# One tile of a 31-tap convolution given to GpSimd, the bias products put among the modulation sums, and another order in the router

## The reference

```python
mod = c_act @ w_ada[l] + b_ada[l]                    # six modulation vectors
u = modulate(rmsnorm(h, g_norm1[l]), sh1, sc1)
y = hybrid_mixer(u, w_in[l], ...)                    # the first mixer
h = h + ga1[:, None, :] * y
u2 = modulate(rmsnorm(h, g_norm2[l]), sh2, sc2)
y2 = hierarchical_moe(u2, ...)

# in hybrid_mixer: a depthwise convolution of 31 taps over 512 channels
a, gt = jnp.split(u, 2, axis=-1)
z = a * jax.nn.sigmoid(gt)
z = lax.conv_general_dilated(z, w_dw, window_strides=(1,), padding=[(CONV_WIDTH - 1, 0)], ...) + b_dw
z = jax.nn.silu(layernorm(z, ln_g, ln_b))

# in hierarchical_moe: 4 groups of 8 experts, the best group, then its best 2 experts
lg = t @ w_rg + b_rg
_, gsel = lax.top_k(lg, 1)
le_sel = jnp.take_along_axis(le, gsel[:, :, None], axis=1)[:, 0, :]
top_v, top_i = lax.top_k(le_sel, TOP_K)
for e in range(N_EXPERTS):
    hid = jax.nn.silu(t @ w1[e]) * (t @ w3[e])
    y = y + comb[:, e:e + 1] * (hid @ w2[e])
```

## Time and profile before

| | before |
|---|---|
| runs | 1441.7 us (1437.92 to 1446.5, three runs) |
| the profiled execution's own time | 1443.55 us |
| its span | 1441.7 us |
| mean granted TensorE clock | 0.92 |
| TensorE, VectorE, ScalarE, GpSimd busy | 1199.7, 675.6, 449.9, 2.2 us |
| read from device memory | 372.03 MB |

### The profile page before, as it was taken

One profiled execution on the slowest core, in us unless ns is written; L12 is line 12 of the kernel. 1 busy time (PEld: TensorE's weight loads), 2 busy tenths in 40 slices (PEclk: granted clock), 3 DMA queues, 4 the chain that ended last, 5 costly groups with the idle time before them and its releaser, 6 DMA issues.

```text
span 1441.7 us, 20119 instructions
## 1 busy us (share of the span) xinstructions
PE 1199.7 (83%) x8634; PEld 947.6 (66%) x8634; DVE 675.6 (47%) x1146; ACT 449.9 (31%) x643; POOL 2.2 (0%) x16
## 2 busy tenths in 40 slices
PE   5999998897865657555675599999998889899998
PEld 2789896686322223222231399899998889899986
DVE  2547987453200101101010464455657786678974
ACT  2543343442000000000000353343545454545453
POOL 0000000000000000000000000000000000000000
PEclk7799999999989879888788999899999999999999
DMA  9797862977999999999999565343443425345552
GB/s 355 253 317 241 278 165 89 360 253 304 420 420 420 420 420 418 420 421 420 420 420 415 201 213 183 108 133 118 148 161 116 142 93 193 115 158 182 190 203 88
DMA packets 169655, 374.48 MB, mean 260 GB/s; under 512 B 8263, under 2 KB 121305, under 8 KB 145881
## 3 DMA queue, kind: packets, MB, share of 16 engines
q1 hardware_dynamic: 167040, 369.55, 69.5%
q0 software_dynamic: 144, 3.54, 0.8%
q10 hardware_dynamic: 2376, 0.04, 0.1%
HBM read 372.03 MB, written 4.62 MB: 261 GB/s over the span
## 4 chain that ended last, share of the span: by engine, by line
PE 58%; DMA 21%; DVE 11%; SPq 5%; ACT 3%; issue 3%; DVEq 0%; ACTq 0%
PE bank L603 31%; DMA arena<-in_w 15%; PE bank L1231 4%; DVE arena L1262 4%; DMA above<-in_w 4%; PE bank L907 4%; SPq L2599 4%; DVE fine L1254 2%; PE bank L947 2%; ACT fine L2059 2%; DVE arena L1254 2%; PE bank L563 2%; PE bank L600 2%; PE bank L634 1%; DVE arena L1259 1%
## 5 line engine op out<-in xcount | busy, mean ns | idle before, releaser
L603 PE MATMUL bank<-fine 128*128 128x256 f32 x4512 | 564.6, 287 | 17.8 <-DVE fine L1254 17.7
L603 PEld LDWEIGHTS bank<-fine 128*128 128x128 f32 x4512 | 554.3, 195 | 31.9 <-issue 27.8
L1254 DVE TENSOR_TENSOR fine<-arena,fine 128x1024 fp32r<-128x1024 f32 (+2 forms) x263 | 299.6, 1168 | 181.5 <-ACT fine L2059 172.1
L2059 ACT ACTIVATE fine<-arena 128x1024 fp32r<-128x1024 f32 (+2 forms) x279 | 266.3, 984 | 197.5 <-PE bank L603 82.4
L2059 ACT ACTIVATE arena<-bank 128x256 f32<-128x256 f32 (+2 forms) x153 | 68.2, 473 | 523.9 <-PE bank L919 191.7
L907 PE MATMUL bank<-arena 128*32 128x512 f32 x640 | 121.6, 790 | 62.8 <-DMA arena<-in_w 41.2
L1254 DVE TENSOR_TENSOR arena<-arena,bank 128x512 f32<-128x512 f32 x8 | 8.4, 1052 | 286.7 <-PE bank L907 286.7
L907 PE MATMUL bank<-above,arena 128*32 128x512 f32 x384 | 75.1, 724 | 51.6 <-issue 21.6
L2059 ACT ACTIVATE arena<-arena 128x512 f32<-128x512 f32 (+6 forms) x90 | 61.1, 708 | 152.1 <-DVE arena L1262 62.2
L907 PEld LDWEIGHTS bank<-arena 128*32 128x32 f32 x640 | 30.4, 140 | 118.9 <-issue 117.3
L1262 DVE SCALAR_TENSOR_TENSOR arena<-arena 128x256 f32<-128x256 f32 (+3 forms) x262 | 107.7, 484 | 1.1 <-ACT arena L2059 0.8
(11 more groups left out here) (177 smaller groups left out, 784.5 us busy)
## 6 DMA issues: line engine op xcount, KB each, us to landing
arena<-in_w SPq DMA_DIRECT2D x118, 1024.0 KB, 26.8
above<-in_w SPq DMA_DIRECT2D x66, 1024.0 KB, 26.5
arena<-in_w_in SPq DMA_DIRECT2D x62, 1024.0 KB, 5.5
arena<-in_w_ada SPq DMA_DIRECT2D x24, 1024.0 KB, 9.8
arena<-in_ffn_w_up SPq DMA_DIRECT2D x22, 1024.0 KB, 5.1
arena<-in_ffn_w_down SPq DMA_DIRECT2D x11, 1024.0 KB, 5.0
arena<-in_w_ada_f SPq DMA_DIRECT2D x8, 1024.0 KB, 10.6
above<-in_w SPq DMA_DIRECT2D x12, 512.0 KB, 18.5
```

Of the source, the lines that this page charges most:

```text
L603: ins = e.matmul(o, w[:, k, j * P:j * P + P], x[:, kt, :], start=start, stop=stop, skip_group_check=True)
L1254: return e.tensor_tensor(o, a, b, f)
L2059: return e.activation(o, i, f, bias=bias, scale=scale)
```

## The change

Three parts. First, `conv_taps` on VectorE has three tiles in place of four, and GpSimd makes the fourth with a product into `rstd` and an addition for each tap. Its DMA of the bias rows stands behind all of that, and TensorE waits for both engines ahead of the layer norm. Second, the router's products are put in another order, the count is made with two instructions ahead of the gather and two behind it, and the wait of L907 is for each quarter of `xg`. Third, the bias products move ahead of `ada_sums(3)`, with their copies and store on ScalarE, and `oh` is loaded with 33 partitions into the place of `u`, between the fourth and the fifth piece of the modulation weights.

```diff
-        oh = shaped(flat(v)[:, 0:1152], 3, 384)
+        oh = shaped(flat(u)[:, 0:1152], 3, 384)
...
             ada_sums(2)
-            ada_sums(3)
-            ada_to_mod(0)
-            advance("q", 2)
             e.wait_ge(*cols_in["first"])
             e.wait_ge(*oh_in[0])
...
                 e.matmul(bank[0:6, 0:384], rtab[0:33, 6 * g:6 * g + 6], oh[0:33, g, :], start=True,
                          stop=True).then_inc(*rep_made.up(g))
+            ada_sums(3)
+            ada_to_mod(0)
+            advance("q", 2)
...
             e.wait_ge(*conv["taps"])
+            e.wait_ge(*conv_g["taps"])
...
-            e.wait_ge(*squares["most"])
-            e.matmul(bank[:, 0:256], ones, sq[:, 0, :], start=True, stop=False)
             e.wait_ge(*route["wr"])
             raw_logits(0)
             raw_logits(1)
+            e.wait_ge(*squares["most"])
+            e.matmul(bank[:, 0:256], ones, sq[:, 0, :], start=True, stop=False)
...
             turn_h(0, 0)
+            turn_h(0, 1)
             bank = misc(route_a, "rstd")
...
-            turn_h(0, 1)
...
-            e.matmul(bank[:, 0:32], before, mask[:, 0, :], start=True, stop=True)
-            e.matmul(bank[:, 32:64], ones, mask[:, 0, :], start=True, stop=False)
-            e.matmul(bank[:, 32:64], before, mask[:, 1, :], start=False, stop=True)
-            e.matmul(bank[:, 64:96], ones, mask[:, 0, :], start=True, stop=False)
-            e.matmul(bank[:, 64:96], ones, mask[:, 1, :], start=False, stop=True).then_inc(*router.up("ranks"))
+            e.matmul(bank[:, 0:64], before, flat(mask), start=True, stop=False, skip_group_check=True)
+            e.matmul(bank[:, 32:64], ones, mask[:, 0, :], start=False, stop=True, skip_group_check=True).then_inc(*router.up("ranks"))
...
             gather_tokens(0, (0,))
+            e.matmul(bank[:, 64:96], ones, mask[:, 0, :], start=True, stop=False, skip_group_check=True)
+            e.matmul(bank[:, 64:96], ones, mask[:, 1, :], start=False, stop=True, skip_group_check=True).then_inc(*router.up("count"))
...
-                            e.wait_ge(*gathered[quad, th])
+                            e.wait_ge(*gathered[quad, th, 0])
                         for k in range(4):
+                            if wn == 0 and k:
+                                e.wait_ge(*gathered[(quad, th, k) if k < 3 else (quad, th)])
...
                 for j in range(1, 31):
-                    for m in range(4):
+                    for m in range(3):
...
+            e.wait_ge(*out_v["a", 1])
+            e.wait_ge(*fills["zp"])
+            e.tensor_scalar(cacc[:, 3, :], zp[:, 3, 0:256], col("w_dw", 3 * 31), col("b_dw", 3), ALU.mult, ALU.add).then_inc(
+                *conv_g.up(0))
+            for j in range(1, 31):
+                e.wait_ge(*conv_g[j - 1])
+                e.tensor_scalar(rstd, zp[:, 3, j:j + 256], col("w_dw", 3 * 31 + j), None, ALU.mult).then_inc(
+                    *conv_g.up(("product", j)))
+                e.wait_ge(*conv_g["product", j])
+                e.tensor_tensor(cacc[:, 3, :], cacc[:, 3, :], rstd, ALU.add).then_inc(
+                    *conv_g.up(j if j < 30 else "taps"))
             e.wait_ge(*row_out[0])
             e.wait_ge(*scores[2, 1])
...
             for j in range(4):
                 ada(j)
+                if j == 1:
+                    e.dma_start(flat(oh)[0:33, :], T["consts"][0:33, NCONST0 + NCONST1:NCONST]).then_inc(*oh_in.up(0, 16))
             load("q", 2)
-            e.wait_ge(*ada_sum[4])
-            e.dma_start(flat(v)[:, 0:1152], T["consts"][:, NCONST0 + NCONST1:NCONST]).then_inc(*oh_in.up(0, 16))
```

More of the change, by code:

```diff
@@ L477, in build @@
             "ffn_silu", "down_x_hi", "ends_by_scalar"))
-        fills = signal("fills")
+        fills, conv_g = signal("fills"), signal("conv_taps_by_gpsimd")
         x_turned, norm_sum, ada_sum, ada_mod, rep_made, products_of, small_made, scores, kd_turned, states, ln_sum, o_made, on_turned, conv_out = (
@@ L1505, in conv_taps @@
                 for j in range(1, 31):
-                    for m in range(4):
+                    for m in range(3):
                         e.wait_ge(*conv[m, j - 1])
                         stt(cacc[:, m, :], zp[:, m, j:j + 256], col("w_dw", m * 31 + j), cacc[:, m, :], ALU.mult, ALU.add).then_inc(
-                            *conv.up((m, j) if j < 30 or m < 3 else "taps"))
+                            *conv.up((m, j) if j < 30 or m < 2 else "taps"))
                     yield
@@ L1689, in gather_tokens @@
                         k = 4 * g + j
-                        ins = ts(xg[:, i, k, :], bank_of(gathered, (quad, g))[:, j * P:j * P + P], perm[:, 0, k:k + 1], ALU.mult,
-                                 perm[:, 1, k:k + 1], ALU.add)
-                    ins.then_inc(*gathered.up((quad, g)))
+                        ts(xg[:, i, k, :], bank_of(gathered, (quad, g))[:, j * P:j * P + P], perm[:, 0, k:k + 1], ALU.mult,
+                           perm[:, 1, k:k + 1], ALU.add).then_inc(*gathered.up((quad, g, j) if j < 3 else (quad, g)))
             e.wait_ge(*perm_in[0])
@@ L1710, in vector_program @@
             step(e.tensor_copy(rank, shaped(ranks[:, 0:64], 2, 32)))
+            e.wait_ge(*router["count"])
             step(e.reduce_max(cnt[:, 0:1], ranks[:, 64:96], AX), "count")
@@ L2177, in scalar_program @@
             norm_rows(0, lambda pair: h_in[1, pair // 2])
+            for g in range(3):
+                e.wait_ge(*rep_made[g])
+                act(rep[0:6, g, :], bank_of(rep_on, g)[0:6, 0:384], ACT.Copy).then_inc(*rep_on.up(g))
+            e.wait_ge(*rep_on[2])
+            e.dma_start(bass.AP(scratch.tensor, P * rows, [[384, 6], [6 * 384, 3], [1, 384]]), rep[0:6, :, :]).then_inc(
+                *row_out.up(0, 16))
             high_half()
@@ L2187, in scalar_program @@
             advance("q", 1)
-            for g in range(3):
-                e.wait_ge(*rep_made[g])
-                act(rep[0:6, g, :], bank_of(rep_on, g)[0:6, 0:384], ACT.Copy).then_inc(*rep_on.up(g))
-            e.wait_ge(*rep_on[2])
-            e.dma_start(bass.AP(scratch.tensor, P * rows, [[384, 6], [6 * 384, 3], [1, 384]]), rep[0:6, :, :]).then_inc(
-                *row_out.up(0, 16))
             e.wait_ge(*ada_sum[7])
```

## The result

The changed kernel takes 1456.72 us (median of 4 runs, 1453.22 to 1461.76), the kernel before 1440.16 (4 runs, 1437.92 to 1446.5). The ratio is 1.0095, 95% interval 1.0067 to 1.0122: **0.7 to 1.2% slower**. The forecast was 1433 us, with a range up to 1449. The profiled execution took 1456.19 us, its span 1454.4, against 1441.7: 12.7 us more.

A forecast was written before the change was run, and what follows sets the result against it. Expert weight loads set the time from 360 us, so earlier savings pass on one to one. Start -3.0, mixer -2.3 and router -3.6 sum to -8.9: 1434.65 us profiled, 1433 predicted as median, range 1426 to 1449.

The forecast's parts named there:

- To land by then it must be issued by 169.7: Mixer: bias-row copy behind GpSimd's chain costs nothing if issued by 169.7 us, before ScalarE's store at 183.97.
- the hold: Convolution: time by which GpSimd's instructions lengthen VectorE's, h us per product-and-addition pair; forecast near 0.41.
- the case with a chance of 0.10: Mixer rival: GpSimd too slow, its copy late; at 1.2 us per instruction store 17 late, +8, 1443 us; chance 0.10.
- the one with 0.27: Mixer rival: GpSimd holds VectorE up for its instructions' length; 1439 us at h 0.62, 1447 at 0.89; chance 0.27.
- The signs that the prediction named: Mixer: TensorE's waits above 15 us mean GpSimd holds VectorE; GpSimd's DMA behind 170 us means its copy is late.
- The mixer: Convolution: VectorE loses 31 instructions, gain 4.5 us if GpSimd hinders nobody; half taken, 2.3 us saved, range -4.5 to +12.
- The formula 30h - 14.7: Convolution: mixer's net change in us if each GpSimd pair holds VectorE up for h us; never below -4.5.
- the 7.5 us of free time: Convolution: VectorE's free time from 113.6 to 141.5 us, expected to absorb 7.5 us of GpSimd's hindrance.
- 9 us in hand: Mixer: TensorE, up to three halves of 3 us behind, absorbs 9 us of the late store, leaving +8.
- The start: Bias products moved earlier let L563 run unbroken, with an earlier clock rise: 3.0 us saved, bounds 0.7 to 5.4.
- the clock rises at 48.3: Start: before, TensorE's clock rose some 4.8 us after L563 ran unbroken from 43.48; now expected near 43.0.
- The router: Before the experts: squares 1.8, count 1.3, single scalings 0.6 us; 3.6 of 3.7 us saved, bounds 1.9 to 4.0.

The follow-up runs named there:

- run 10: Kernel before, all four tiles on VectorE, nothing computed by GpSimd; only its copy of the bias rows waits for level 3's last tap: 1456.51 us, ratio 1.0095.
- run 2: Changed kernel with GpSimd's copy of the bias rows issued ahead of its tap 14, not behind tap 30: 1439.2 us, ratio 0.9979.
- run 1: Changed kernel with all four convolution tiles back on VectorE, new start and router kept: 1435.49 us, ratio 0.9958.
- run 4: Kernel before with only the fourth tile moved to GpSimd and the copy issued ahead of the 14th pair: 1446.73 us, ratio 1.0034.
- run 6: Kernel before, all taps on VectorE; GpSimd also computes the fourth tile's 61 instructions into free tiles, copy after its 13th pair: 1460.96 us, ratio 1.0137.
- run 7: Kernel before, all taps on VectorE; GpSimd also runs 61 chained clearings of free tiles, which read nothing: 1443.2 us, ratio 1.0.
- run 8: Kernel before with only the start's part of the change: 1442.24 us, ratio 0.9996.
- run 3: Kernel before with only the fourth tile moved to GpSimd and the copy behind its 61 instructions: 1466.11 us, ratio 1.016.
- run 5: Changed kernel with ScalarE's store going to its own piece of scratch, so that it waits for no copy: 1457.22 us, ratio 1.0109.
- run 11: Kernel before, all taps on VectorE, GpSimd's copy in time, then its overwritten products, additions and plain copies beside levels 1 to 3: 1449.28 us, one run.

## Why the prediction was wrong

**What failed** is the step that put GpSimd's chain and the copy behind it at nothing: "To land by then it must be issued by 169.7 ... 0.92 us per instruction with its wait. Below that it costs nothing", and against it "a clearing takes 0.3 us". The sum of the forecast has no term for the late copy; run 10, which has the late copy and nothing else, is 13.9 us slower. An instruction took 1.17 us with its wait, and the copy went out at 182.27. A product took 0.93 to 0.98 us undisturbed or beside the taps, an addition 0.64, with 0.08 to 0.10 between them: 1.75 to 1.79 us for a pair, 0.90 us for an instruction at most, which would have been just in time. What made it 1.17 is VectorE's other forms, beside which a product took up to 2.83 us: the hold works in both directions. So the case with a chance of 0.10 came true, and with it the one with 0.27, since reading side by side drives both. I had treated them as alternatives. The signs that the prediction named for them were there: 22.1 us of TensorE's waits (15 was the mark) and GpSimd's DMA behind 170.

**The mixer: -2.3 forecast, +18.9 in the trace.** Its terms:

- *The hold.* The formula 30h - 14.7 came near, the h of 0.41 was too low. With 0.60 from the taps it gives +3.3 us; the medians show 3.7 (run 2 less run 1) and 3.6 (run 4). In run 6, where nothing is taken off VectorE, 30 x 0.60 less the 7.5 us of free time would be 10.5. TensorE's three waits there, 14.3 us, are 11.3 more than the 3.0 that it had before, so this part is about right. But 17.5 us were measured. TensorE ran at the low clock behind each wait, where 48, 24 and 24 products took 1.5, 2.4 and 1.5 us more than at the high one: 5.4. Together that is 16.7, and from the end of L563 to the layer norm (L786) the trace is 16.8 us longer than run 7's. The formula had no term for the clock.
- *The late copy.* The rival's lateness was right: for 1.2 us per instruction it had the store 17 us late, and against 183.97 - 2.97 = 181.0 it came 17.7 late. Its price, +8, was too small, because of the "9 us in hand". Run 10 shows 0.2 us: the products that TensorE had ahead were just used up when the store was due. In the changed kernel TensorE waited 13.6 of the 17.7 us only because the hold, with its clock, had by then made it 4.0 us late itself, and the low clock behind the wait cost another 2.4. Runs 2, 4 and 10 put the whole at 17.5, 19.4 and 13.9 us, the last with the copy 4.4 us earlier than in the changed kernel.
- *The gain that was to be had.* Of level 5's wait 1.6 us were to go. It fell from 5.85 to 4.28.

**The start: -3.0 forecast, -2.97 in the trace, but -1.2 us by medians (run 8).** The unbroken L563 and the rise inside it came as described. What was wrong is the reference: I read "the clock rises at 48.3" as a property of the kernel before, and it was one draw, the slower of two. That the two traces then differed by just 2.97 us is luck. Against the six faster ones, whose mean is 45.9, the new start's mean of 45.8 saves next to nothing; the interval of run 8, 3.8 us faster to 2.6 slower, can't say more.

**The router: -3.6 forecast, -4.28 in the trace.** The squares gave 1.9 (1.8 forecast), the count 1.3 (1.3) and the single scalings 1.0 (0.6). Alone it is 2.6 us by medians, with an interval from 5.8 faster to 0.1 slower; between runs 8 and 1, which differ by the router, the ratio falls from 0.9996 to 0.9958, 5.5 us.

**The sum.** By medians the steps are -7.7 for start and router (run 1), +3.7 for the hold (run 2 less run 1) and +17.5 for the copy (the changed kernel less run 2). They come to 13.6 by construction, since each is the difference of neighbours in one row of runs; the sum is no check. The prices of the copy that come from other runs, 19.4 (runs 3 and 4) and 13.9 (run 10), give 15.4 and 9.9 in place of 13.6; the ratio of 1.0095 is 13.7 us. So the copy is by far the largest term, and its size is known to some 3 us.

One slip in reading: it is slices 10 to 21 that lie in 360 to 792 us, and TensorE stands at 8 in slice 10 and at 7 in slice 9. No term rests on it.

## What to carry to other kernels

A queue is part of an engine's program: before work is put on an idle engine, list what it issues behind that work and when each piece is due, and price that as the first term, not as a rival. An unexplained wait is not settled by removing its semaphore (run 5): ask what else the waiting transfer shares with the one in flight. Work "in hand" is counted at the moment when the late thing is due, not by how far an engine may run ahead. And where TensorE's clock rises in one trace is one draw; a term that rests on it needs several.

## What the runs showed of the hardware

- On GpSimd, at 128 x 256 in f32, a product with one tile input took 0.93 us at best, an addition with two 0.64, a plain copy 0.40, a clearing 0.31. The product with a column of scalars took longer than the addition, which I had not expected. For the addition the Trainium skill, "GPSIMD Engine Reference", section 3.1, had led to an estimate of 0.56; the measurement is 0.64.
- VectorE's unbroken taps and the additions behind them kept one product of GpSimd's waiting from 141.02 to 147.73, until a form with an operand in `bank` came (146.84, run 11); in run 6 a product got in among such taps at once. Once GpSimd's chain is between VectorE's taps, the two alternate, at 0.60 us per tap in place of 0.40.
- A product held VectorE up by about 0.2 us, an addition by 0.4, a plain copy by 0.14, a clearing not at all (runs 11 and 7).
- A store of two times 4 KB took 10.5 to 12.5 us to land with no copy in flight (before, changed kernel, run 10) and 27.2 beside a copy of 3.5 MB that had been issued 3.6 us before it and weight loads (run 5).
